# Attention in a two-layer streaming trunk: padded meta transpose and block meta values

## The reference, cut to what matters

```python
km, vm = k[:, :N_META], v[:, :N_META]
s_meta = einsum('bcqkgd,bmkd->bcqkgm', qr, km)      # 16 meta keys, seen by every query
s_win = einsum('bcqkgd,bcnkd->bcqkgn', qr, kw)      # this chunk and the one before: 128 keys
p = sink_softmax(concatenate([s_meta, s_win], -1), sk)
o_r = einsum('bcqkgm,bmkd->bcqkgd', p[..., :N_META], vm) \
    + einsum('bcqkgn,bcnkd->bcqkgd', p[..., N_META:], vw)
```

## Time and profile before

| | |
|---|---|
| median of 3 runs | 1167.52 us (1163.15 to 1168.8) |
| span of the profiled execution | 1165.8 us |
| PE busy | 1125.1 us, 97% of the span |
| DVE busy | 540.5 us, 46% |
| ACT busy | 472.4 us, 41% |
| POOL busy | 172.8 us, 15% |
| attention blocks, layer 0 | 84.4 to 149.6 us |
| attention blocks, layer 1 | 651.2 to 718.1 us |

### The profile page before, as it was taken

How to read it: one execution, slowest core, us unless ns; L and a number is a source line. 1 busy time by engine, 2 the same in 40 slices (tenths; PEclk the granted TensorE clock), 3 DMA queues, 4 the chain that set the end, 5 groups by cost and what they waited for, 6 DMA issues and landing times.

```text
span 1165.8 us, 21588 instructions
## 1 busy us (share of the span) xinstructions
PE 1125.1 (97%) x8850; PEld 1082.5 (93%) x8850; DVE 540.5 (46%) x663; ACT 472.4 (41%) x652; POOL 172.8 (15%) x138
## 2 busy tenths in 40 slices
PE   4899899999999999999969999999999999999997
PEld 3897699999999999999969876999999999999997
DVE  4666646445454545212157565455544554432222
ACT  3675524544444443111238643353434343421110
POOL 2362003000100010000043510121100110000000
PEclk9989989999999999999989897999999999999999
DMA  5211032322232232233221112223232323233211
GB/s 197 89 46 37 1 109 73 109 73 92 88 108 72 80 100 90 73 100 97 75 74 47 37 37 69 76 74 109 73 107 72 108 72 108 72 100 93 70 63 72
DMA packets 92828, 94.47 MB, mean 81 GB/s; under 512 B 3712, under 2 KB 91096, under 8 KB 92776
## 3 DMA queue, kind: packets, MB, share of 16 engines
q1 hardware_dynamic: 91728, 93.01, 25.0%
q10 hardware_dynamic: 1048, 0.76, 0.2%
HBM read 91.65 MB, written 2.10 MB: 80 GB/s over the span
## 4 chain that ended last, share of the span: by engine, by line
PE 92%; DVE 4%; ACT 2%; issue 2%; DMA 1%; SPq 0%; DVEq 0%; ACTq 0%
PE slot L429 83%; PE slot L573 2%; PE slot L576 2%; DVE x_lo L1009 2%; PE slot L544 1%; PE slot L555 1%; PE slot L481 1%; PE slot L464 1%; DMA x_in<-in_x 1%; DVE ms_work L1075 1%; PE slot L558 1%; DVE sink_all L999 0%; PE slot L667 0%; DVE v_T L1047 0%; ACT rot_s L815 0%
## 5 line engine op out<-in xcount | busy, mean ns | idle before, releaser
L429 PE MATMUL slot<-x_hi,w_hi 128*128 128x264 f32 x1728 | 368.7, 290 | 18.0 <-DVE x_lo L1009 17.9
L429 PE MATMUL slot<-x_lo,w_hi 128*128 128x264 f32 x1728 | 364.0, 288 | 0.0
L429 PE MATMUL slot<-x_hi,w_lo 128*128 128x264 f32 x1728 | 363.9, 288 | 0.0
L343 DVE TENSOR_TENSOR w_lo<-raw,w_hi 128x2048 fp32r<-128x2048 f32 (+2 forms) x86 | 192.8, 2242 | 252.6 <-ACT w_hi L334 252.6
L429 PEld LDWEIGHTS slot<-x_hi,w_hi 128*128 128x128 f32 x1728 | 276.5, 191 | 23.1 <-DVE x_lo L1009 20.7
L334 ACT ACTIVATE w_hi<-raw 128x2048 fp32r<-128x2048 f32 (+3 forms) x90 | 162.6, 1806 | 304.6 <-PE slot L429 297.0
L429 PEld LDWEIGHTS slot<-x_lo,w_hi 128*128 128x128 f32 x1728 | 275.3, 191 | 0.0
L429 PEld LDWEIGHTS slot<-x_hi,w_lo 128*128 128x128 f32 x1728 | 275.0, 191 | 0.0
L429 PE MATMUL slot<-m_hi,w_hi 128*128 128x264 f32 x704 | 143.0, 284 | 0.0
L429 PE MATMUL slot<-m_lo,w_hi 128*128 128x264 f32 x704 | 142.9, 284 | 0.0
L429 PE MATMUL slot<-m_hi,w_lo 128*128 128x264 f32 x704 | 142.6, 284 | 0.0
(11 more groups left out here) (137 smaller groups left out, 1085.8 us busy)
## 6 DMA issues: line engine op xcount, KB each, us to landing
raw<-in_w_gate SPq DMA_DIRECT2D x44, 512.0 KB, 4.4
raw<-in_w_up SPq DMA_DIRECT2D x44, 512.0 KB, 4.6
raw<-in_w_down SPq DMA_DIRECT2D x32, 512.0 KB, 4.0
raw<-in_w_in SPq DMA_DIRECT2D x20, 512.0 KB, 4.8
raw<-in_w_out SPq DMA_DIRECT2D x16, 512.0 KB, 4.0
raw<-in_w_down SPq DMA_DIRECT2D x16, 384.0 KB, 3.5
x_in<-in_x SPq DMA_DIRECT2D x4, 512.0 KB, 5.7
out<-y_out SPq DMA_DIRECT2D x8, 256.0 KB, 2.9
```

Of the source, the lines that this page charges most:

```text
L343: ins = nc.vector.tensor_tensor(w_lo[s][:, a:b], raw[s][:, a:b], w_hi[s][:, a:b].bitcast(f32), ALU.subtract)
L429: ins = nc.tensor.matmul(out_half, w[ws][:, r, cols], a[:, k, half * HALF:(half + 1) * HALF], start=first and n == 0 and w is w_hi and a i ...
```

## The change

The four meta probability tiles of a block are written by DVE into a zeroed buffer of 128 columns, 32 columns to a head, and go through one transpose; the result is copied out as 128 rows by 128. The meta values stand four times in a zeroed 128 by 128 block for each key head, so that one matmul for each key head gives the meta part of all 128 output rows. The window matmuls are ordered so that one with output rows 0 to 63 alternates with one with 64 to 127, and the scores matmuls so that j2 alternates. ACT fills the value blocks with four copies in place of one; POOL clears both buffers once a layer.

```diff
-            v_meta = sb(sc, "v_meta", [N_META, P])
+            v_meta = sb(sc, "v_meta", [P, N_KV_HEADS, P])
+            probs_pad = sb(sc, "probs_pad", [P, 2, P])
-            probs_meta = sb(sc, "probs_meta", [N_META, 2, 4 * P])
+            probs_meta = sb(sc, "probs_meta", [P, 2, P])
 scores:
-                    for t in range(4):
-                        j2, kv = divmod(t, 2)
+                    for kv, j2 in ((0, 0), (0, 1), (1, 0), (1, 1)):
 probs_T:
+                    if b == 0:
+                        pe.wait_ge(probs_zero, l + 1)
+                    ins = nc.tensor.transpose(slot[s][:, 1, 0:P], probs_pad[:, b % 2], ident)
                     for t in range(4):
-                        ins = nc.tensor.transpose(slot[s][0:N_META, 1, t * P:(t + 1) * P],
-                                                  probs[:, b % 2, t, 0:N_META], ident)
 heads:
+                    for kv in range(N_KV_HEADS):
+                        ins = nc.tensor.matmul(slot[s][:, 0, kv * P:(kv + 1) * P], v_meta[:, kv],
+                                               probs_meta[:, b % 2], start=kv == 0, stop=n == 0 and kv == 1,
+                                               skip_group_check=True)
+                    for kv, j2 in ((0, 0), (0, 1), (1, 0), (1, 1)):
+                        t = j2 * 2 + kv
-                        ins = nc.tensor.matmul(dst, v_meta[:, dims], probs_meta[:, b % 2, cols],
-                                               start=True, stop=n == 0)
                         if n > 0:
                             (window matmul as before, start=False, stop=kv == 1)
 POOL, once a layer:
+                nc.gpsimd.memset(v_meta[:], 0.0).then_inc(vmeta_zero, 1)
+                nc.gpsimd.memset(probs_pad[:], 0.0).then_inc(probs_zero, 1)
 ACT, values:
-                nc.scalar.activation(v_meta[:], flat[0:N_META, NWIN * P:(NWIN + 1) * P], ACT.Copy)
+                act.wait_ge(vmeta_zero, l + 1)
+                for t in range(4):
+                    j2, kv = divmod(t, 2)
+                    nc.scalar.activation(v_meta[t * META_ROWS:t * META_ROWS + N_META, kv,
+                                                j2 * HEAD_DIM:(j2 + 1) * HEAD_DIM], ..., ACT.Copy)
 divide, DVE:
-                    nc.vector.tensor_tensor(probs[:, y, :, 0:nk], probs[:, y, :, 0:nk],
-                                            rden[:, y]... , ALU.mult)
+                    ins = nc.vector.tensor_tensor(probs_pad[:, y]...[:, :, 0:N_META],
+                                                  probs[:, y, :, 0:N_META], rden[:, y]..., ALU.mult)
+                    if nk > N_META:
+                        ins = nc.vector.tensor_tensor(probs[:, y, :, N_META:nk], probs[:, y, :, N_META:nk],
+                                                      rden[:, y]..., ALU.mult)
 probs_out(0) on ACT and meta_probs_out on DVE:
-                    ... probs_meta[:, b % 2], slot[pt][0:N_META, 1, :]
+                    ... probs_meta[:, b % 2], slot[pt][:, 1, 0:P]
```

More of the change, by code:

```diff
@@ L43 @@
 NWIN = NCH - 1
+META_ROWS = P // 4
 U_KV, U_Q, U_U23, U_U01, U_POOL, U_OUT = 0, 1, 3, 4, 5, 6
@@ L228, in build_trunk @@
         meta_out = sem("meta_out")
+        vmeta_zero, probs_zero = sem("vmeta_zero"), sem("probs_zero")
         mixhi_ready = sem("mixhi_ready")
@@ L568, in heads @@
                         pe.wait_ge(meta_out, l * (NB - 1) + b)
-                    for t in range(4):
-                        j2, kv = divmod(t, 2)
-                        dst = slot[s][j2 * HEAD_DIM:(j2 + 1) * HEAD_DIM, 0, kv * P:(kv + 1) * P]
+                    for kv in range(N_KV_HEADS):
[4 more added lines that the diff above has]
+                        t = j2 * 2 + kv
                         dims, cols = slice(kv * HEAD_DIM, (kv + 1) * HEAD_DIM), slice(t * P, (t + 1) * P)
-                        ins = nc.tensor.matmul(dst, v_meta[:, dims], probs_meta[:, b % 2, cols],
-                                               start=True, stop=n == 0)
                         if n > 0:
-                            ins = nc.tensor.matmul(dst, v_win[0:n, max(b - 2, 0), dims], probs_win[0:n, b % 2, cols],
-                                                   start=False, stop=True)
+                            ins = nc.tensor.matmul(slot[s][j2 * HEAD_DIM:(j2 + 1) * HEAD_DIM, 0, kv * P:(kv + 1) * P],
+                                                   v_win[0:n, max(b - 2, 0), dims], probs_win[0:n, b % 2, cols],
+                                                   start=False, stop=kv == 1, skip_group_check=True)
                     ins.then_inc(filled[s], 1)
@@ L852, in _ @@
                 flat = slot[s][:].rearrange("p a t -> p (a t)")
-                nc.scalar.activation(v_meta[:], flat[0:N_META, NWIN * P:(NWIN + 1) * P], ACT.Copy)
+                act.wait_ge(vmeta_zero, l + 1)
+                for t in range(4):
+                    j2, kv = divmod(t, 2)
+                    nc.scalar.activation(v_meta[t * META_ROWS:t * META_ROWS + N_META, kv,
+                                                j2 * HEAD_DIM:(j2 + 1) * HEAD_DIM],
+                                         flat[0:N_META, NWIN * P + kv * HEAD_DIM:NWIN * P + (kv + 1) * HEAD_DIM],
+                                         ACT.Copy)
                 nc.scalar.activation(v_win[:, 0:4].rearrange("p w d -> p (w d)"), flat[:, 0:4 * P], ACT.Copy)
@@ L905, in probs_out @@
                     else:
-                        ins = nc.scalar.activation(probs_meta[:, 0], slot[pt][0:N_META, 1, :], ACT.Copy)
+                        ins = nc.scalar.activation(probs_meta[:, 0], slot[pt][:, 1, 0:P], ACT.Copy)
                     ins.then_inc(evac[pt], 1)
@@ L1136, in divide @@
                     ch.link(nc.vector.reciprocal(rden[:, y], den[:, y]))
-                    nc.vector.tensor_tensor(probs[:, y, :, 0:nk], probs[:, y, :, 0:nk],
-                                            rden[:, y].unsqueeze(2).broadcast_to([P, 4, nk]), ALU.mult)\
-                      .then_inc(probs_ready, 1)
+                    if b == 0:
+                        dve.wait_ge(probs_zero, l + 1)
+                    ins = nc.vector.tensor_tensor(probs_pad[:, y].rearrange("p (t m) -> p t m", t=4)[:, :, 0:N_META],
+                                                  probs[:, y, :, 0:N_META],
+                                                  rden[:, y].unsqueeze(2).broadcast_to([P, 4, N_META]), ALU.mult)
+                    if nk > N_META:
+                        ins = nc.vector.tensor_tensor(probs[:, y, :, N_META:nk], probs[:, y, :, N_META:nk],
+                                                      rden[:, y].unsqueeze(2).broadcast_to([P, 4, nk - N_META]),
+                                                      ALU.mult)
+                    ins.then_inc(probs_ready, 1)
                 def meta_probs_out(b):
@@ L1144, in meta_probs_out @@
                     dve.wait_ge(filled[pt], ps.before(f"probs_T{b}", l) + 1)
-                    nc.vector.tensor_copy(probs_meta[:, b % 2], slot[pt][0:N_META, 1, :]).then_inc(meta_out, 1)
+                    nc.vector.tensor_copy(probs_meta[:, b % 2], slot[pt][:, 1, 0:P]).then_inc(meta_out, 1)
                 def heads_lo(b):
```

## The result

| | us |
|---|---|
| before | 1167.35 median of 4 runs (1163.15 to 1168.8) |
| after | 1140.83 median of 4 runs (1140.1 to 1142.01) |
| ratio | 0.9774, 95% interval 0.9747 to 0.98 |
| forecast | 1151.2, range 1142 to 1160 |
| profiled span, before and after | 1165.8 and 1138.2 |

The change gives 26.5 us where 16.3 were forecast, and the time lies under the range.

A forecast was written before the change was run, and what follows sets the result against it. PE was taken to bound the blocks, leading the softmax round by 1.5 us a step. Rounds 6.7 plus tail 2.3 less side rows 0.4 give 8.6 a layer, 17.2 less 0.9: 16.3, so 1151.2 us, range 1142 to 1160.

The forecast's parts named there:

- Heads, scores, transposes on PE: PE work per block: heads 1.16 us against 2.88, scores unchanged at 0.77, three fewer transposes worth 0.33 us.
- The cause, a change of form: In heads on PE, each change between the 16-row and the 128-row matmul form costs 0.14 us.
- The bound after the change: In the blocks, the closed softmax round of ACT and DVE sets the pace; PE waits 1 to 2 us a step.
- PE stays the bound or nearly: Rival: the round is shorter than reckoned, up to 34.0 us come off, time 1134 to 1144; chance 0.09.
- The size of the round: ACT and DVE softmax round: 5.4 us becomes 5.6 with the split product; exps(4) to exps(8) takes 24.3 us, 6.7 less.
- the 0.4 set aside for side rows: Side rows also wait for DVE's copy of a finished side tile: two at 0.2 us each, 0.4 back a layer.
- what was gained ahead of exps(4): Rounds up to exps(4) are near 6 us and bound by the chain; nothing is gained there.
- The tail, the step that failed: From exps(8) to the last pool map, one line through divide(8), transposes, meta copy, heads_lo(7), heads(8): 2.3 us less.
- I count neither its end nor its return: Half clock in heads(8), 1.34 us more than heads(2), left out of the sum; PE may meet it elsewhere.
- The rival that the clock would fall in the rounds: PE's waits bring 1.2 GHz steps: a few more give 1158 to 1165, chance 0.09; many, over 1165, chance 0.05.
- ACT's copies: Four value copies in place of one ahead of `v_win` on ACT: +0.45 us a layer, +0.9 in all.

The follow-up runs named there:

- order alone: Kernel before with the four meta matmuls of each heads block put first and the window ones behind them, same shapes and count: 1141.89 us, ratio 0.9766.
- form alone: Changed kernel with meta values as four 128 by 64 matmuls, the window matmul of the same rows right behind each: 1140.04 us, ratio 0.9756.
- the filled kernels: Unread matmuls added in PE's waits at the layer's start and ahead of heads(7) and heads(8): changed kernel 1137.54 us, kernel before 1160.6 us.

## Why the prediction was wrong

- **Heads, scores, transposes on PE: right.** 1.12 us against 1.16; scores the same; five transposes, 0.11 apart.
- **The cause, a change of form: right,** shown by order alone and by form alone. The sum also had the pairing of the window matmuls behind it, the other half of what heads gained.
- **The bound after the change: right.** The chain of softmax, heads_hi, heads_lo, divide and row maxima is closed, while PE waits up to 1.1 us at a time in the rounds, fewer and smaller waits than forecast. The measured time falls among those of the rival "PE stays the bound or nearly" (1134 to 1144, chance 0.09), but not by its mechanism.
- **The size of the round: too long.** 5.6 was forecast, and 5.18 is the round with nothing inserted. I had added durations end to end with 0.05 between. In the rows heads_hi starts 0.11 before the accumulator's end and den 0.08 before the end of heads_lo, and the split product costs 0.07, not 0.17 (den to sink_arg is 2.48 us, it was 2.41). From exps(4) to exps(8) it was 23.3 and 23.1 us instead of 24.3, and the 0.4 set aside for side rows didn't come; what was gained ahead of exps(4), 0.1 and 0.6 us, I had put at zero. In both layers that is 3.7 us.
- **The tail, the step that failed: 2.3 us a layer forecast, 4.6 and 6.4 measured.** It has two parts. heads(7) was left out: I read the line through divide(8), but its transposes waited 0.94 us for PE behind heads(7). At full clock, as the filled kernels have it, the tail went from 10.2 to 6.9, so 3.3 us a layer and not 2.3. The rest, 1.3 and 3.2 us, is the clock of these two profiles.
- **The half clock, "I count neither its end nor its return": the term that should have been in the sum.** The prediction held that PE, idler, may meet it elsewhere. Little came back where PE ends last: in the two profiles the tails and the output projections have some 20 us of 1.2 GHz before (from 146, 706 and 716 us) and some 3 us after (from 691). By the medians of the filled kernels this is worth 2 to 4 us of the 26.5, by their ratios up to 6. The rival that the clock would fall in the rounds is wrong: 0.94 and 0.96 in the blocks.
- **ACT's copies: priced too low,** 0.72 us a layer ahead of `v_win` for the 0.45 forecast.

Rounds 3.7, tails 2.0 at full clock, clock 2 to 4, less 0.5 for the copies: 7 to 9 of the 10.2 us that were missed. The 1 to 3 that remain lie within what medians and clock leave open. The range ended at 1142, and so it had no room for the round, the tail and the clock erring the same way at once.

## What to carry to other kernels

Group matmuls by form before anything is padded or merged: here a reordered loop gives as much as new buffers, copies and block matmuls do, half of it by fewer changes of form and half because neighbours of one form with different output halves pair. In a tail, follow each engine's queue backwards as well as the data; the work ahead of the waiting instruction may be on the path. Where a row shows the half clock on work that ends last, its cost belongs in the sum, and a few matmuls put into the waits ahead of it can give it back; where another engine ends last, expect little from it, and look where the half clock goes instead.

## What the runs showed of the hardware

- A change between a matmul of 16 and one of 128 contracted rows costs 0.14 us. Sixteen instructions take 2.88 us with eight changes and no pairs, 1.52 with one change and half of them paired, and 1.19 with two changes and all in pairs. A change from 128 by 128 to 128 by 64 isn't free either: four turns of 0.11 are 0.44 us, and the window matmuls start 0.53 after the meta ones (111.17, 111.70).
- Matmuls with output rows 0 to 63 and 64 to 127 run two at a time in either order (scores 0.76 and 0.77 us), and one can start ahead of another that stands before it in the program.
- 44 added matmuls made the kernel before 9.0 us shorter; the mean granted clock of its runs went from between 0.976 and 0.985 to between 0.986 and 0.992.
- Four ACT copies of 16 by 64 out of PSUM take 0.87 us, one of 16 by 128 0.25.
